# Thirty-two experts written out instead of looped, expert 1's two selections side by side, and the order of the products around gate2

## The chip, the cores and the metric

One Trainium2 chip, one of its cores. The metric is the time of one execution on the device in microseconds (us). The kernel before ran at a median of 1014.62 us over 3 runs (1013.69 to 1019.47).

## What is computed

One layer of an encoder on two requests of 256 tokens with 1024 channels (512 tokens together), all in float32. The part that matters here is its second half, a mixture of 32 experts (4 groups of 8): each token goes to the best group, and in it to the two best experts.

```python
def expert_block(args):
    xb, e = args
    return (jax.nn.silu(xb @ w_exp_gate[e]) * (xb @ w_exp_up[e])) @ w_exp_down[e]
...
x = _ln_affine(ALPHA * x + gate2 * f, ln2_g, ln2_b)
```

`w_exp_gate[e]` and `w_exp_up[e]` are 1024 x 512, `w_exp_down[e]` is 512 x 1024: 2 MB each, 6 MB for an expert, read once for each of the 32. `gate2` is a vector for each request, from its conditioning; the kernel multiplies it into the experts' results.

## The kernel before

The program is written out by hand for each engine; engines wait for each other by semaphores. After the token mixer come the router and then the experts, one after another.

**Router.** TensorE (PE) makes the router's logits (products of 36 columns), then four products of the two gate2 rows (2 rows deep, 512 columns wide) into banks 5 and 1, then `keep_clock(2)`: two full 128x128 products of 512 columns whose result nobody reads. It then waits for VectorE's (DVE's) one-hot matrix `both`, and counts, with small products, which slot of its expert each token takes. From that DVE makes `slot_of`, and from it `sel`: 0/1 matrices for a pair of experts, by which products gather an expert's up to 64 tokens.

**An expert** on PE: `gate_up` (16 products of 64 rows into bank 0, gate in the upper half, up in the lower), then `selected` (8 products that gather half of the channels of a pair of later experts into bank 2), `h_transposes` of the hidden rows, `x_transposes` of the gathered rows, then `down` (8 products into bank 1). ScalarE (ACT) applies the silu, copies `x_rows` and `hid_t` out of the banks; DVE multiplies gate by up, copies `x_t`, writes `sel` for the next pair and scales the result by gate2 (`yout`); GpSimd (POOL) stores it to `round_y`. Expert 0 gathers with float32 products (`selected_alone`). Expert 1 gathers the first half of pair (2, 3) beside its `gate_up` and the second half after its `down`, all through bank 2.

**Further rounds.** An expert may have more than 64 tokens. Behind each expert every engine reads two values from `tab` and branches over a body (`further_rounds`, on PE line 961) that is a whole second expert. With these inputs one expert of the 32 takes it.

**Loops.** PE and DVE write out experts 0 to 5, run `Fori(1, 5)` over bodies of six (experts 6 to 29; PE's loop is line 985), and write out 30 and 31. SyncE (SP) does the same from expert 6 on, ACT loops over bodies of three from expert 3, POOL over three from 0. Because a tile can't be indexed by the loop's register everywhere, DVE moves the columns of `n0` and `slot_of` down by six at the end of each body (`next_columns`, lines 1849 to 1853).

**Weights.** SP issues the loads in order. There are three buffers for gate and up, two for down:

```python
def next_gate_up(e, s):
    ...
    sp.wait_ge(m_sem["gum"], e - 2)      # gate_up of expert e-3 is done
def next_down(e, d):
    ...
    sp.wait_ge(m_sem["ym"], e - 1)       # down of expert e-2 is done
```

Both also wait until a further round of that expert is through with the buffer. Behind the loop the order is `next_down(29)`, then gate and up and down of 30, then of 31.

Of the kernel before, what the change touches and what calls it, by code (L numbers as in the profile page):

```python
# [10 lines left out]
TILES = TOK // 128  # L11
# [28 lines left out]
def hybrid_encoder(nc, x_prompt, x_sample, c_prompt, c_sample, w_mod, b_mod, w_in, b_in, w_spatial,  # L40
# [12 lines left out]
    with ctx:  # L53
# [78 lines left out]
        n0_next = at("n0_next", [128, NEXP], f32, S0 + 3072)  # L132
# [49 lines left out]
        slot_next = at("slot_next", [128, NEXP, TILES], f32, T0 + 35328)  # L182
# [174 lines left out]
        def _(sp):  # L357
# [85 lines left out]
        def _(pool):  # L443
# [150 lines left out]
        def _(pe):  # L594
# [288 lines left out]
            def down(ht, d, bank, sm):  # L883
                for fc in range(FC):
                    mm(bank[0:CAP, :], ht[:, fc, :], down_w[d][:, fc, 0:512], start=(fc == 0), stop=(fc == FC - 1))
                    x = mm(bank[CAP:128, :], ht[:, fc, :], down_w[d][:, fc, 512:1024], start=(fc == 0), stop=(fc == FC - 1))
                x.then_inc(sm["ym"], 1)

            def expert(e, k, turn, last=False, turns=None):

                s, d, a = k % 3, k % 2, k % 2
                opening = isinstance(e, int) and e == 0
                second = isinstance(e, int) and e == 1
                chooses = not (isinstance(e, int) and e >= NEXP - 2)
                loaded = 32 * (2 * turn + k // 3 + 1)
# [4 lines left out]
                pe.wait_ge(m_sem["xt"], e + 1 if opening or second else e - a + 2)  # L900
# [6 lines left out]
                if opening:  # L907
                    selected_alone(1, B[2]).then_inc(m_sem["xs"], 1)
                elif second:
                    pe.wait_ge(dve_h2lo, TILES)  # L910
                    pe.wait_ge(m_sem["sl"], 2)
                    selected(sel, B[2], 0).then_inc(m_sem["xs"], 1)
                elif chooses:
                    pe.wait_ge(m_sem["xt"], e + 2)
                    if a == 0:
                        pe.wait_ge(m_sem["sl"], 3 * turn + k // 2 + 2)
# [3 lines left out]
                if chooses:  # L920
                    pe.wait_ge(m_sem["xr"], e + 2 if opening or second else e + 3)
                    x_transposes(x_rows, B[2]).then_inc(m_sem["xtr"], 1)
                pe.wait_ge(m_sem["ht"], e + 1)
                pe.wait_ge(e_dn[d], 16 * (3 * turn + k // 2 + 1))
                if opening:
# [9 lines left out]
                if opening:  # L935
                    pe.wait_ge(dve_rt, 2)
# [7 lines left out]
            def further_rounds(e, s, d, more, first):  # L944

                def further_round(turns):
# [12 lines left out]
                    down(hid_t_x, d, B[5], x_sem)  # L959
# [30 lines left out]
            expert(30, 0, 5)  # L990
            expert(31, 1, 5, last=True, turns=last_turns)
# [21 lines left out]
        def _(act):  # L1013
# [218 lines left out]
            def rows_in(count):  # L1232
                act.wait_ge(m_sem["xs"], count)
                copy(x_rows[:, :], B[2][:, :]).then_inc(m_sem["xr"], 1)

            rows_in(1)
# [30 lines left out]
            def expert(e, turns=None):  # L1267

                opening = isinstance(e, int) and e == 0
                second = isinstance(e, int) and e == 1  # L1270
                chooses = not (isinstance(e, int) and e >= NEXP - 2)
                if opening:
                    act.wait_ge(dve_rt, 2)
                gate_silu(m_sem, B[0], sg_hid, e, 0)
                if chooses:
                    rows_in(e + 2 if opening or second else e + 3)
# [6 lines left out]
                if opening:  # L1283
# [6 lines left out]
            for k in range(3):  # L1290
                expert(k)
            with act.Fori(1, 10) as t:
                for k in range(3):
                    expert(3 * t + k)
# [46 lines left out]
        def _(dve):  # L1341
# [373 lines left out]
            def chosen_rows(out, column):  # L1715
                return dve.tensor_tensor(out[:, :, :], slots_by_tile(TILES),
# [4 lines left out]
            chosen_pair(sel, slot_of[:, 0:2, :]).then_inc(m_sem["sl"], 1)  # L1721
# [79 lines left out]
            def last_chunks(count):  # L1801
# [3 lines left out]
                columns_in(x_t[:, 1:4:2, :, :], B[2]).then_inc(m_sem["xt"], 1)  # L1805

            def expert(e, k, turn, turns=None):
                s = k % 3
                opening = isinstance(e, int) and e == 0
                second = isinstance(e, int) and e == 1  # L1810
                chooses = not (isinstance(e, int) and e >= NEXP - 2)
                dve.wait_ge(m_sem["silu"], e + 1)
                dve.tensor_tensor(sg_hid[CAP:128, :], B[0][CAP:128, :], sg_hid[0:CAP, :], ALU.mult).then_inc(m_sem["hid"], 1)  # L1813
                if opening:
# [5 lines left out]
                if s == 0:  # L1820
                    dve.tensor_scalar(side[:, 0, 0:3], n0[:, k:k + 3], -0.5, None, ALU.is_gt).then_inc(dve_g, 1)
                    dve.tensor_scalar(side[:, 1, 0:3], n0[:, k:k + 3], -0.5, None, ALU.is_le).then_inc(dve_g, 1)
                if not (isinstance(e, int) and e < 3):
                    dve.wait_ge(y_st[s], 32 * (2 * turn + k // 3))
                gate_of_slots(yout[s], dve_g, 20 * turn + 2 * (k // 3 + 1) + 2 * k, side[:, 0, s:s + 1], side[:, 1, s:s + 1])
                if opening:
                    dve.wait_ge(m_sem["xtr"], 2)
                    columns_in(x_t[:, 2:4, :, :], B[2]).then_inc(m_sem["xt"], 1)
                    chosen_pair(sel, slot_of[:, 2:4, :]).then_inc(m_sem["sl"], 1)
                elif second:  # L1830
                    first_chunks(3)
                elif chooses and k % 2 == 0:
                    first_chunks(e + 3)
                elif chooses:
                    last_chunks(e + 3)
                    chosen_pair(sel, slot_of[:, k + 3:k + 5, :]).then_inc(m_sem["sl"], 1)
                if opening:
                    for i in range(TILES):
                        dve.wait_ge(act_h2hi, i + 1)
                        dve.tensor_tensor(h2_lo[i][:, :, :], h2[i][:, :, :], h2_hi[i][:, :, :].bitcast(f32), ALU.subtract).then_inc(dve_h2lo, 1)  # L1840
                dve.wait_ge(m_sem["ym"], e + 1)
# [4 lines left out]
                further_rounds(k, *(turns or turns_of(e)))  # L1846

            def next_columns(turn):
                dve.tensor_copy(n0_next[:, 0:NEXP - 6], n0[:, 6:NEXP]).then_inc(dve_g, 1)
                dve.tensor_copy(slot_next[:, 0:NEXP - 6, :], slot_of[:, 6:NEXP, :]).then_inc(dve_g, 1)  # L1850
                dve.wait_ge(dve_g, 20 * turn + 18)
                dve.tensor_copy(n0[:, 0:NEXP - 6], n0_next[:, 0:NEXP - 6]).then_inc(dve_g, 1)
                dve.tensor_copy(slot_of[:, 0:NEXP - 6, :], slot_next[:, 0:NEXP - 6, :]).then_inc(dve_g, 1)
                dve.wait_ge(dve_g, 20 * turn + 20)

            for k in range(6):
                expert(k, k, 0)
            next_columns(0)
            with dve.Fori(1, 5) as t:
                for k in range(6):  # L1860
# [3 lines left out]
            expert(30, 0, 5)  # L1864

            chosen_rows(is_last, 1).then_inc(dve_sel, 1)
# [66 lines left out]
            expert(31, 1, 5, turns=last_turns)  # L1933
# [63 lines left out]
```

## Time and profile before

| | |
|---|---|
| profiled execution, device time | 1015.61 us |
| its span, first to last instruction | 1013.6 us |
| mean granted TensorE clock | 0.965 of full speed |
| PE matmul busy | 929.8 us (92%) |
| instructions / DMA moved | 12645 / 297.89 MB |
| token mixer and router | to about 465 us |
| experts 0 to 30 | 470.68 to 968.57 us |
| gather, last expert, layer norm, output | to 1013.6 us |

Times in rows are us from the start of the span. "issue" in the chain of waits is time in which the engine waited for nothing that the profile shows. A PE record is half of a float32 product, so 16 products show as 32 records. PEld is TensorE's weight load, and a row PEldq is an instruction of TensorE's sequencer (register work, branches). The queue q8 "instruction" carries blocks of 16 KB of program code.

### The profile page before, as it was taken

How to read it: one execution, taken by the hardware profiler on the slowest of the kernel's cores; microseconds unless marked ns; L12 is line 12 of the kernel's file. 1: busy time of each engine (PE TensorE's matmuls, PEld its weight loads, DVE VectorE, ACT ScalarE, POOL GpSimd, SP SyncE). 2: the span in 40 equal slices, each digit the busy share in tenths (PEclk: the TensorE clock that was granted, in tenths of full speed). 3: DMA queues.
4: the chain of work that ended last, by engine and by line, in shares of the span. 5: the costliest groups of instructions: out<-in, count | busy, mean ns of one | idle time of the engine just before them, and what ended most of it. 6: DMA issues, size and time to landing. Idle time of an engine off the chain costs nothing.

```text
span 1013.6 us, 12645 instructions
## 1 busy us (share of the span) xinstructions
PE 929.8 (92%) x4235; PEld 543.9 (54%) x4236; DVE 384.9 (38%) x683; ACT 244.3 (24%) x355; POOL 113.7 (11%) x174
## 2 busy tenths in 40 slices
PE   3789999999999999998999999799978899889984
PEld 2457677888888887883444344244334244344331
DVE  4522343565343257885422222222223032122235
ACT  2322243441334244363211011010010011011014
POOL 2210267000002000000000000000000000000031
PEclk9789999999999999998999999899989999899998
DMA  9884653365647525457989999999996599998953
GB/s 368 316 276 153 237 208 130 119 233 187 239 173 214 178 83 172 119 202 324 419 350 429 425 426 428 420 431 424 427 413 267 209 428 429 378 405 361 421 210 124
DMA packets 46635, 297.89 MB, mean 294 GB/s; under 512 B 4418, under 2 KB 6562, under 8 KB 30946
## 3 DMA queue, kind: packets, MB, share of 16 engines
q1 hardware_dynamic: 36352, 263.99, 64.7%
q0 software_dynamic: 9600, 31.18, 9.1%
q10 hardware_dynamic: 610, 1.66, 0.6%
q8 instruction: 57, 0.93, 0.4%
q14 instruction: 16, 0.13, 0.0%
HBM read 275.81 MB, written 21.00 MB: 293 GB/s over the span
## 4 chain that ended last, share of the span: by engine, by line
PE 84%; issue 4%; ACT 3%; DMA 3%; SPq 2%; DVE 2%; POOL 0%; DVEq 0%; POOLq 0%; ACTq 0%
PE bank L596 81%; DMA modraw<-in_w_mod 2%; PE bank L864 2%; SPq L372 2%; ACT x_rows L1015 2%; DMA y_first<-round_y,pos_y 1%; DVE wo_lo L1559 0%; PE bank L653 0%; DMA round_y<-yout 0%; ACT w_hi L1015 0%; POOL y_second L584 0%; POOL y_first L584 0%; DVE g_a L1576 0%; PE bank L880 0%; ACT L1141 0%
## 5 line engine op out<-in xcount | busy, mean ns | idle before, releaser
L596 PE MATMUL bank<-gate_w,x_t 128*64 128x512 f32 x512 | 234.0, 610 | 28.2 <-issue 26.3
L596 PE MATMUL bank<-up_w,x_t 128*64 128x512 f32 x512 | 234.4, 611 | 0.0
L596 PEld LDWEIGHTS bank<-gate_w,x_t 128*64 128x64 f32 x512 | 71.3, 141 | 176.6 <-issue 176.6
L596 PE MATMUL bank<-h_hi,w_hi 128*128 128x512 f32 x320 | 127.0, 397 | 1.6 <-ACT h_hi L1049 1.6
L596 PE MATMUL bank<-h_hi,w_lo 128*128 128x512 f32 x320 | 126.8, 396 | 0.0
L596 PE MATMUL bank<-h_lo,w_hi 128*128 128x512 f32 x320 | 125.5, 400 | 0.0
L596 PE MATMUL bank<-down_w,hid_t 128*64 128x512 f32 x512 | 116.9, 598 | 1.0 <-ACT hid_t L1015 0.9
L1813 DVE TENSOR_TENSOR sg_hid<-bank,sg_hid 64x512 f32<-64x512 f32 x32 | 22.2, 694 | 244.3 <-ACT sg_hid L1244 244.3
L1244 ACT ACTIVATE sg_hid<-bank 64x512 f32<-64x512 f32 x33 | 19.6, 592 | 376.0 <-PE bank L596 376.0
L1394 DVE TENSOR_TENSOR w_lo<-raw,w_hi 128x1024 fp32r<-128x1024 f32 x56 | 68.6, 1227 | 79.2 <-ACT w_hi L1015 79.1
L596 PEld LDWEIGHTS bank<-h_lo,w_hi 128*128 128x128 f32 x320 | 60.6, 189 | 25.3 <-issue 11.7
L538 POOL DMA_DIRECT2D round_y<-yout x31 | 16.0, 517 | 511.8 <-issue 511.8
L1015 ACT ACTIVATE w_hi<-raw 128x1024 fp32r<-128x1024 f32 x56 | 58.9, 1053 | 54.3 <-PE bank L596 51.6
L596 PEld LDWEIGHTS bank<-up_w,x_t 128*64 128x64 f32 x512 | 71.0, 141 | 0.0
L596 PEld LDWEIGHTS bank<-h_hi,w_hi 128*128 128x128 f32 x320 | 61.7, 193 | 14.3 <-ACT h_hi L1049 2.0
L596 PEld LDWEIGHTS bank<-h_hi,w_lo 128*128 128x128 f32 x320 | 61.4, 192 | 13.3
L596 PEld LDWEIGHTS bank<-down_w,hid_t 128*64 128x64 f32 x512 | 34.8, 136 | 60.4 <-issue 56.2
L1842 DVE TENSOR_TENSOR yout<-bank,yout 128x512 f32<-128x512 f32 x32 | 22.1, 691 | 82.8 <-PE bank L596 82.8
L596 PE MATMUL bank<-h_hi,sel 128*128 128x512 f32 x120 | 50.3, 419 | 0.0
L596 PE MATMUL bank<-a_lo,w_hi 128*128 128x512 f32 x128 | 49.9, 390 | 0.3 <-DVE w_lo L1394 0.3
L596 PE MATMUL bank<-a_hi,w_lo 128*128 128x512 f32 x128 | 49.8, 389 | 0.0
L596 PE MATMUL bank<-a_hi,w_hi 128*128 128x512 f32 x128 | 49.8, 389 | 0.0
(322 smaller groups left out, 1125.6 us busy)
## 6 DMA issues: line engine op xcount, KB each, us to landing
down_w<-in_w_exp_down SPq DMA_DIRECT2D x32, 2048.0 KB, 15.3
gate_w<-in_w_exp_gate SPq DMA_DIRECT2D x31, 2048.0 KB, 12.2
up_w<-in_w_exp_up SPq DMA_DIRECT2D x31, 2048.0 KB, 17.4
modraw<-in_w_mod SPq DMA_DIRECT2D x24, 1024.0 KB, 8.6
raw<-in_w_in SPq DMA_DIRECT2D x9, 2048.0 KB, 9.9
round_y<-zrow POOLq DMA_DIRECT2D x6, 2048.0 KB, 7.6
raw<-in_w_branch_b SPq DMA_DIRECT2D x2, 2048.0 KB, 9.4
raw<-in_w_branch_a SPq DMA_DIRECT2D x2, 2048.0 KB, 10.3
```

What stands on the lines that cost most here:

```text
L372: sp.dma_start(modraw0[m][:, :, :], mod_source(m)).then_inc(s_m0[m], 16)
L538: pool.dma_start(round_y[bass.ds(row, rows), 0:512], y[0:rows, :]).then_inc(done, 16)
L596: return pe.matmul(out, lhsT, rhs, start=start, stop=stop, skip_group_check=True)
L864: x = pe.transpose(bank[:, 128 * k:128 * k + 128], rows[:, 128 * k:128 * k + 128], ident)
L1015: return act.activation(out, in_, ACT.Copy, scale=scale)
L1244: act.activation(sgb[0:CAP, :], bank[0:CAP, :], ACT.Silu).then_inc(sm["silu"], 1)
L1394: dve.tensor_tensor(w_lo[par][:, :, :], raw[:, u % 2, :, 128 * (b % 4):128 * (b % 4) + 128], w_hi[par][:, :, :].bitcast(f32), ALU.subtract ...
L1813: dve.tensor_tensor(sg_hid[CAP:128, :], B[0][CAP:128, :], sg_hid[0:CAP, :], ALU.mult).then_inc(m_sem["hid"], 1)
L1842: dve.tensor_tensor(yout[s][:, :], B[1][:, :], yout[s][:, :], ALU.mult).then_inc(m_sem["yo"], 1)
```

## The change

All engines write out experts 0 to 29 one by one, with constants in place of register arithmetic; `next_columns` and its two spare tiles go. Expert 1 gathers both halves of its pair beside `gate_up`, the second into bank 6, and the transposes of the second half stand in the middle of its `down`. The first `sel` is written in two halves, so that expert 0's is there first. On PE `keep_clock(2)` moves ahead of the gate2 products, and `keep_clock(1)` stands behind them.

```diff
# SP
-            for e in range(3, 6):
+            for e in range(3, NEXP - 2):
                 next_gate_up(e, e % 3)
                 next_down(e - 1, (e - 1) % 2)
-            with sp.Fori(1, 5) as t:
-                for k in range(6):
-                    next_gate_up(6 * t + k, k % 3)
-                    next_down(6 * t + k - 1, (k + 1) % 2)
# POOL
-            with pool.Fori(0, 10) as t:
-                for k in range(3):
-                    expert(3 * t + k, k)
+            for e in range(NEXP - 2):
+                expert(e, e % 3)
# PE
+            keep_clock(2)
             for r, bank in enumerate((B[5], B[1])):
                 for c in range(2):
                     j = 2 + c
                     x = mm(bank[64 * c:64 * c + 64, :], cst[...], modrow[...])
             x.then_inc(pe_lg, 1)
-            keep_clock(2)
+            keep_clock(1)
             pe.wait_ge(dve_rt, 1)
...
-                elif second:
+                elif e == 1:
                     pe.wait_ge(dve_h2lo, TILES)
-                    pe.wait_ge(m_sem["sl"], 2)
+                    pe.wait_ge(m_sem["sl"], 3)
                     selected(sel, B[2], 0).then_inc(m_sem["xs"], 1)
+                    selected(sel, B[6], 1).then_inc(m_sem["xs"], 1)
...
-                down(hid_t, d, B[1], m_sem)
-                if second:
-                    pe.wait_ge(m_sem["xt"], 3)
-                    selected(sel, B[2], 1).then_inc(m_sem["xs"], 1)
+                down(hid_t, d, B[1], range(FC // 2))
+                if e == 1:
                     pe.wait_ge(m_sem["xr"], 4)
-                    x_transposes(x_rows, B[2]).then_inc(m_sem["xtr"], 1)
+                    x_transposes(x_rows, B[6]).then_inc(m_sem["xtr"], 1)
+                down(hid_t, d, B[1], range(FC // 2, FC)).then_inc(m_sem["ym"], 1)
...
-            for k in range(6):
-                expert(k, k, 0)
-            with pe.Fori(1, 5) as t:
-                for k in range(6):
-                    expert(6 * t + k, k, t)
+            for e in range(NEXP - 2):
+                expert(e)
# ACT, expert 1
-                if second:
-                    rows_in(4)
+                if e == 1:
+                    act.wait_ge(m_sem["xtr"], 3)
+                    rows_in(4, B[6])
# DVE
-            chosen_pair(sel, slot_of[:, 0:2, :]).then_inc(m_sem["sl"], 1)
+            for a in range(2):
+                chosen_rows(sel[:, :, a, :], a).then_inc(m_sem["sl"], 1)
...
+                elif e == 1:
+                    first_chunks(3)
+                    last_chunks(4, B[6])
+                    next_pair(4)
...
                 dve.tensor_tensor(yout[s][:, :], B[1][:, :], yout[s][:, :], ALU.mult).then_inc(m_sem["yo"], 1)
-                if second:
-                    last_chunks(4)
-                    chosen_pair(sel, slot_of[:, 4:6, :]).then_inc(m_sem["sl"], 1)
...
-            with dve.Fori(1, 5) as t:
-                for k in range(6):
-                    expert(6 * t + k, k, t)
-                next_columns(t)
```

## Rows read from the trace of the kernel before

**Rows 1.** The page: the DMA engines' busy tenths in 40 slices of the span

```profile
DMA  9884653365647525457989999999996599998953
```

**Rows 2.** The chain that ended last, from 440 us: start us, us, what

```profile
496.39 5.63 PE bank L596 x24
...
589.94 1.86 issue
591.80 9.14 PE bank L596 x40
...
616.13 12.50 PE bank L596 x56
...
629.96 12.51 PE bank L596 x56
...
647.39 6.18 issue
653.57 11.78 PE bank L596 x40
...
741.80 6.30 issue
748.11 10.63 PE bank L596 x40
...
774.65 3.61 PE bank L596 x16
...
859.79 5.96 issue
865.75 11.51 PE bank L596 x40
```

**Rows 3.** Branches of TensorE's sequencer: lines 961 and 985, ns min/median/max

```profile
L961 PEldq COMPARE_BRANCH  x32: 77/320/4337, 484.0 to 978.0; - x32
...
L985 PEldq COMPARE_BRANCH  x4: 76/7446/7641, 645.7 to 952.9; - x4
```

**Rows 4.** DMA queue of program blocks, 645 to 652 us: packets, MB, share

```profile
q8 instruction: 2, 0.03, 3.4%
```

**Rows 5.** DMA queue of the weights, 515 to 742 us: packets, MB, share

```profile
q1 hardware_dynamic: 6405, 93.36, 96.8%
```

**Rows 6.** SP's issues of the loads for down of experts 10 and 19

```profile
606.17 0.33 SPq L392 DMA_DIRECT2D down_w<-in_w_exp_down  x1
...
742.11 0.33 SPq L392 DMA_DIRECT2D down_w<-in_w_exp_down  x1
```

**Rows 7.** Us to landing of the loads issued at 513.55, 742.11, 860.10

```profile
gate_w<-in_w_exp_gate SPq DMA_DIRECT2D x1, 2048.0 KB, 7.7
...
down_w<-in_w_exp_down SPq DMA_DIRECT2D x1, 2048.0 KB, 22.9
...
down_w<-in_w_exp_down SPq DMA_DIRECT2D x1, 2048.0 KB, 17.4
```

**Rows 8.** The first products of experts 1 and 2

```profile
485.96 0.59 PE L596 MATMUL bank<-gate_w,x_t 128*64 128x512 f32 x1
...
504.53 0.61 PE L596 MATMUL bank<-gate_w,x_t 128*64 128x512 f32 x1 [1.17 <-DVE x_t L1761]
```

**Rows 9.** The router on PE and DVE, in order of time

```profile
456.53 2.72 PE L596 MATMUL bank<-modrow,cst 2*64 2x512 f32 x8
459.18 3.78 PE L596 MATMUL bank<-cst 128*128 128x512 f32 x4
...
461.52 0.29 DVE L1698 TENSOR_TENSOR both<-q,q 128x128 bf16<-128x128 f32 x1
...
464.07 0.69 DVE L1711 TENSOR_TENSOR sel<-slots,slot_of 128x512 fp32r<-128x512 f32 x1
```

**Rows 10.** Two stretches: us, PE, PEld, DVE, ACT, POOL, clock, DMA, GB/s

```profile
456.50:459.20 2.70, 2.70 (x10) 0.49 (x9) 2.25 (x11) 0.00 (x0) 0.00 (x0) 0.69 1.01 431
...
504.50:508.00 3.50, 3.47 (x10) 1.31 (x12) 0.19 (x1) 0.00 (x0) 0.00 (x0) 0.62 0.99 397
```

More of the change, by code:

```diff
@@ L881, in h_transposes, with down, expert @@
                 x.then_inc(sm["htr"], 1)
-            def down(ht, d, bank, sm):
-                for fc in range(FC):
+            def down(ht, d, bank, chunks):
+                for fc in chunks:
                     mm(bank[0:CAP, :], ht[:, fc, :], down_w[d][:, fc, 0:512], start=(fc == 0), stop=(fc == FC - 1))
                     x = mm(bank[CAP:128, :], ht[:, fc, :], down_w[d][:, fc, 512:1024], start=(fc == 0), stop=(fc == FC - 1))
[L887 to L895, printed above, removed]
+                return x
+            def expert(e, last=False, turns=None):
+                s, d, a = e % 3, e % 2, e % 2
+                loaded = 32 * (e // 3 + 1)
                 if last:
@@ L899, in expert @@
                     pe.wait_ge(e_gu[s], loaded)
-                pe.wait_ge(m_sem["xt"], e + 1 if opening or second else e - a + 2)
+                pe.wait_ge(m_sem["xt"], e + 1 if e < 2 else e - a + 2)
                 gate_up(x_t[:, 2 * a:2 * a + 2, :, :], s, B[0], m_sem, halves=(e_gu[s], loaded) if last else None)
@@ L919, in expert @@
                 h_transposes(sg_hid, B[3], m_sem)
-                if chooses:
-                    pe.wait_ge(m_sem["xr"], e + 2 if opening or second else e + 3)
+                if e < NEXP - 2:
+                    pe.wait_ge(m_sem["xr"], e + 2 if e < 2 else e + 3)
                     x_transposes(x_rows, B[2]).then_inc(m_sem["xtr"], 1)
                 pe.wait_ge(m_sem["ht"], e + 1)
-                pe.wait_ge(e_dn[d], 16 * (3 * turn + k // 2 + 1))
-                if opening:
+                pe.wait_ge(e_dn[d], 16 * (e // 2 + 1))
+                if e == 0:
                     pe.wait_ge(act_rt, 2 * TILES + 1)
@@ L1267, in expert @@
             def expert(e, turns=None):
[L1269 to L1272, printed above, removed]
+                if e == 0:
                     act.wait_ge(dve_rt, 2)
                 gate_silu(m_sem, B[0], sg_hid, e, 0)
-                if chooses:
-                    rows_in(e + 2 if opening or second else e + 3)
+                if e < NEXP - 2:
+                    rows_in(e + 2 if e < 2 else e + 3, B[2])
                 if turns is not None:
@@ L1282, in expert @@
                 hid_columns(m_sem, B[3], hid_t, e)
-                if opening:
+                if e == 0:
                     for i in range(TILES):
                         copy(h2_hi[i][:, :, :], h2[i][:, :, :]).then_inc(act_h2hi, 1)
-                if second:
-                    rows_in(4)
+                if e == 1:
+                    act.wait_ge(m_sem["xtr"], 3)
+                    rows_in(4, B[6])
                 further_rounds(*(turns or turns_of(e)))
[L1290 to L1294, printed above, removed]
+            for e in range(NEXP - 2):
+                expert(e)
             last_turns = turns_of(NEXP - 1)
@@ L1804, in last_chunks, with next_pair, expert @@
                 dve.wait_ge(m_sem["xtr"], count)
[L1805 to L1811, printed above, removed]
+                columns_in(x_t[:, 1:4:2, :, :], bank).then_inc(m_sem["xt"], 1)
+            def next_pair(first):
+                if first < NEXP:
+                    chosen_pair(sel, slot_of[:, first:first + 2, :]).then_inc(m_sem["sl"], 1)
+            def expert(e, turns=None):
+                s = e % 3
                 dve.wait_ge(m_sem["silu"], e + 1)
                 dve.tensor_tensor(sg_hid[CAP:128, :], B[0][CAP:128, :], sg_hid[0:CAP, :], ALU.mult).then_inc(m_sem["hid"], 1)
-                if opening:
+                if e == 0:
                     dve.wait_ge(dve_rt, 2)
@@ L1820, in expert @@
                 if s == 0:
[L1821 to L1826, printed above, removed]
+                    w = min(3, NEXP - e)
+                    dve.tensor_scalar(side[:, 0, 0:w], n0[:, e:e + w], -0.5, None, ALU.is_gt).then_inc(dve_g, 1)
+                    dve.tensor_scalar(side[:, 1, 0:w], n0[:, e:e + w], -0.5, None, ALU.is_le).then_inc(dve_g, 1)
+                if e >= 3:
+                    dve.wait_ge(y_st[s], 32 * (e // 3))
+                gate_of_slots(yout[s], dve_g, 2 * (e // 3 + 1) + 2 * e, side[:, 0, s:s + 1], side[:, 1, s:s + 1])
+                if e == 0:
                     dve.wait_ge(m_sem["xtr"], 2)
                     columns_in(x_t[:, 2:4, :, :], B[2]).then_inc(m_sem["xt"], 1)
[L1829 to L1837, printed above, removed]
+                    next_pair(2)
                     for i in range(TILES):
@@ L1840, in expert @@
                         dve.tensor_tensor(h2_lo[i][:, :, :], h2[i][:, :, :], h2_hi[i][:, :, :].bitcast(f32), ALU.subtract).then_inc(dve_h2lo, 1)
+                elif e == 1:
+                    first_chunks(3)
+                    last_chunks(4, B[6])
+                    next_pair(4)
+                elif e < NEXP - 2 and e % 2 == 0:
+                    first_chunks(e + 3)
+                elif e < NEXP - 2:
+                    last_chunks(e + 3, B[2])
+                    next_pair(e + 3)
                 dve.wait_ge(m_sem["ym"], e + 1)
                 dve.tensor_tensor(yout[s][:, :], B[1][:, :], yout[s][:, :], ALU.mult).then_inc(m_sem["yo"], 1)
-                if second:
-                    last_chunks(4)
-                    chosen_pair(sel, slot_of[:, 4:6, :]).then_inc(m_sem["sl"], 1)
[L1846 to L1854, printed above, removed]
-            for k in range(6):
-                expert(k, k, 0)
-            next_columns(0)
-            with dve.Fori(1, 5) as t:
-                for k in range(6):
-                    expert(6 * t + k, k, t)
-                next_columns(t)
+                further_rounds(e, *(turns or turns_of(e)))
+            for e in range(NEXP - 2):
+                expert(e)
             last_turns = turns_of(NEXP - 1)
-            expert(30, 0, 5)
-            chosen_rows(is_last, 1).then_inc(dve_sel, 1)
+            expert(30)
+            chosen_rows(is_last[:, :, :], NEXP - 1).then_inc(dve_sel, 1)
             dve.wait_ge(dve_sel, 1)
```

29 lines of the change are left out of this document (14 added, 15 removed).

## The prediction

> **What bounds the kernel now.** I read the page first, for where the DMA is full: its line stands at 9 tenths over nearly all of the expert stage, except for two slices at 760 to 811 us [rows 1]. Then the chain of waits over that stage: it is TensorE (PE) from end to end. One expert to the next takes 629.96 - 616.13 = 13.83 us where nothing disturbs it, and at 647.39, 741.80 and 859.79 PE stands still for 6.18, 6.30 and 5.96 us for nothing that the chain can name [rows 2]. These are the starts of experts 12, 18 and 24, each the first of a turn of PE's loop. The view of PE's sequencer names the cause: four branches at line 985 with a median of 7446 ns, the shortest 76 ns, which is the last one, that falls out of the loop [rows 3]; and two blocks of program code move on queue 8 just after the first of them [rows 4]. The jump back throws away the code that was fetched, and PE waits for it while its own queue runs dry. The work behind each stop is slow as well: 40 records take 11.78, 10.63 and 11.51 us where they take 9.14 behind the shorter stop at 589.94 [rows 2].
>
> Last, the weights. The stretch 515 to 742 us carries 93.36 MB on the weight queue [rows 5], 411 GB/s. An expert is three matrices of 2.097 MB, 6.29 MB, so the queue needs 15.3 us for each, more than PE's 13.83. PE is ahead of its supply, and the lag shows in the landing times, which grow while PE runs undisturbed. The stops of the loop are rests in which the supply catches up. So removing them pays only as far as the weights allow; that is the main question of this forecast.
>
> **The change part by part.** First what PE would save if the weights were always there.
>
> - Three jumps back: 6.18 + (11.78 - 9.14) = 8.8, 6.30 + (10.63 - 9.14) = 7.8 and 5.96 + (11.51 - 9.14) = 8.3 us, together 24.9 [rows 2]. Experts 0 to 5 are written out already, and in their stretch the DMA is full too; no stop of this kind stands there.
> - Forward branches over the further rounds stay, 32 of them: median 320 ns, longest 4337 [rows 3]. The one that is long at 587.9 gives the stop of 1.86 us at expert 8 [rows 2]. There are three such (experts 8, 14, 26), at one place of the loop's body, so they hang on where a block of code ends. Written out, an expert's code is a little over a block (one block of code is fetched per expert), so the place drifts, and I expect about as many, 3. Taken at 0; bounds: 3 fewer, -6 us, and 6 more, +12.
> - Expert 1: its first product starts at 485.96, that of expert 2 at 504.53, 18.57 us later [rows 8]. Beside the usual 13.83 it must hold eight more products and four transposes: the chain has `down` and the eight products of a selection at 496.39 in 5.63 us and `down` alone at 774.65 in 3.61, so these take 2.0; and the 1.33 us between 616.13 + 12.50 and 629.96 hold one ACT copy and one set of transposes, 0.7 each [rows 2]. So 16.5, a saving of 2.1. The transposes in the middle of `down` wait for ACT's copy of 0.7 us; half of `down` (1.8 us) and the wait for `hid_t` cover it, without that cover it costs 0.7. ACT's copy queues behind `hid_columns`; DVE's two column copies and the next `sel` (0.69) queue ahead of `yout`, while the second half of `down` runs, and expert 2 doesn't wait.
> - The wait of 1.17 us there is followed by a granted clock of 0.62 [rows 8, 10]: expert 2's products take 1.5 us longer than usual. With no wait this goes: 1.5.
> - The first `sel` in halves: between nothing and half of 0.69 us [rows 9]; 0.3 taken. The second half hides behind `selected_alone` of 3.65 us.
> - `keep_clock`: the gate2 records take 2.72 us at a granted clock of 0.69, so 1.9 at full; the four wide records (two products) behind them take 3.78 [rows 9, 10], at half clock as I read it, so 1.9 at full. If the clock holds, two wide products, the gate2 products and one wide one end at 456.5 + 1.9 + 1.9 + 0.9 = 461.2, before `both` at 461.81 [rows 9], and the counting starts right behind that, some 0.8 earlier than now, where it waits for the wide products to end near 462.9. If the clock falls anyway, 1.9 us of wide work less a part at full, 3.8 and 1.9 end at about 465: 2.2 later. A third way: it holds, but PE is then idle from 461.2 and the clock falls under `selected_alone`, 3.65 us that could take up to 7.3. Wide work ahead of the thin is nearest to the first case, so I take 0.8 saved, bounds 0.8 saved and 3.4 lost.
> - `next_columns` (four small copies on DVE) and the loops of ACT, POOL and SP: nothing, none is on the chain; DVE's copies hide in the 6 us stop. ACT's and DVE's branches show no long stop, in the loops or in the first experts.
>
> Together 24.9 + 2.1 + 1.5 + 0.3 + 0.8 = 29.6 us on PE.
>
> Now what the weights take back. The buffer for `down` is the tight one. Expert 10's load was issued at 606.17 and its `down` began at 629.96: 23.8 us is all that an undisturbed PE leaves [rows 2, 6]. The load for expert 19 was issued at 742.11 and took 22.9, so it landed at 765.0; its `down` began at 774.65 [rows 2, 6, 7]. That is a margin of 9.6 us only, and the DMA was full from 515 us until then. Full, it can't deliver earlier, except by what it rested before: the load of 513.55 landed after 7.7 us, into an empty queue [rows 7]; the trough before it is worth some 3 to 4 us, and the stream starts 1.1 earlier with the router and `sel`. Say 4.4, all of what expert 1 and 2 give. So expert 19 can't begin its `down` before 760.6: a gain of 14.0 us at that point, where PE alone would have 0.3 + 0.8 + 2.1 + 1.5 + 8.8 + 7.8 = 21.3. The queue takes back 7.3, in waits of up to 15.3 - 13.83 = 1.5 us before `down` from about expert 13 on.
>
> Expert 19 has the further round, a second pass of PE without new weights, and the lag clears there (the two light slices of [rows 1]). After it only the jump at expert 24 is left, 8.3. The load issued at 860.10 lands after 17.4 [rows 7]; without the stop the lag grows by 1.5 a time to about 22 at the loads for 29, under 23.8. So 8.3 less 0 to 1, 8.1 taken. The loads for 30 and 31 come in their old order behind `down` of 27 and 28 and are about due when needed. The tail from expert 30's result on is unchanged.
>
> Sum: 14.0 + 8.1 = 22.1 us. 1015.61 - 22.1 = 993.5; the profiled execution is 1.0 over the median of the runs, so 992.5.
>
> The jump is where a page and the trace are weighed. What I read in the rows is a jump that costs 7.4 us and fetches two blocks. The Trainium skill, Runtime: NRT & Kernel Launch, "Instruction fetch mechanics", says the same of a taken branch whose target is outside the fetched window, but gives TensorE's buffer as 128 KiB, or 2048 instructions. By that size a loop of six experts, at about one block of 16 KB each, would sit in the buffer, the stops would have another cause, and only 4.7 us would be gained; by the rows it is 22.
>
> **The rivals.**
>
> *The supply is faster than I think.* The margin at expert 19 assumes that nothing in the 765.0 us is slack; landing times include sharing with the stores. If the queue gives way, PE's whole 29.6 shows: 1014.6 - 29.6 = 985. Against it: 411 GB/s held over 227 us.
>
> *Forward branches stall oftener.* Nine more than before would cost 9 x 1.9 = 17 us, of which the seven before the further round fall into time that the weights take anyway. Left: 22.1 - some 8 = 14, giving 1000.5. For it: the branch over a block's end in the full queue took up to 4.3 us; against it: none of the first six.
>
> *The stops are not the jumps* but something at each sixth expert that stays. Then only 0.3 + 0.8 + 2.1 + 1.5 = 4.7 are gained: 1010. Against it: the branch that falls out of the loop takes 76 ns.
>
> *Slower than before:* the same forward branches, at nearly every expert. PE saves 29.6; to lose 0.5% (5 us) it takes 34.6 / 1.9 = 18 stops in the 24 new experts, 1020. The first six written-out experts speak against it.
>
> **How the numbers follow.** Chances: the forecast (weights take back 4 to 10 us) 0.62, faster supply 0.15, more stalls 0.14, stops stay 0.05, slower 0.02, and 0.02 for anything else that adds. A measurement tells 0.5%, 5 us, from no change: below 1009.5 is faster. The stops-stay case lies at that edge and counts as same for most of its chance. Faster 0.93, same 0.04, slower 0.03. The time is 992.5. Range 985 to 1003: down to the faster supply, and up by the router's 3.4 + 0.8, and by three further stalls after the further round, 6.
>
> **What would show it right or wrong.** The three stops of 6 us are gone and no branch takes 7 us. Between experts 13 and 19 PE waits for `down_w`, the landing times stand near 24 to 27 us there, and expert 19's `down` starts near 760. Expert 1 to 2 takes 16.5 us, with the clock at 1.00. The clock over the gate2 products is 1.00, or the router is wrong. It is wrong if the DMA moves clearly more than 411 GB/s on the weight queue, if long branches at 961 number ten, or if DVE or ACT now stop for code.

## The result and the profile after

The changed kernel ran at a median of 985.17 us (985.11 to 988.54, 4 runs) where the kernel before ran at 1014.42 (4 runs); the ratio is 0.9709, 95% interval 0.9672 to 0.9747. It is faster by 29.3 us, not by the 22.1 of the forecast: 7.3 us under the predicted 992.5, at the low end of its range. Its profiled execution took 985.14 us, its span is 983.4.

**Where it ends up.** The page's line of DMA busy tenths, against [rows 1]: the rest at 760 us is now one slice and not two.

```profile
DMA  9984663346465623809899999999999599999973
```

The chain of waits of the changed kernel, against [rows 2] (of the piece at 794.59 only the start counts here, its window ends soon after):

```profile
509.09 12.50 PE bank L589 x56
...
578.25 3.58 PE bank L589 x16
581.84 1.96 issue
583.80 10.84 PE bank L589 x40
...
678.99 0.27 issue
679.25 6.23 PE bank L589 x28
685.48 1.21 issue
686.69 6.59 PE bank L589 x28
...
698.20 3.48 issue
701.68 12.12 PE bank L589 x40
...
756.65 3.61 PE bank L589 x16
...
794.59 1.43 PE bank L589 x5
...
932.90 5.38 PE bank L589 x16
```

The stops of 6 us are gone. Two smaller ones stand at experts 8 and 16, both with slow work behind them (10.84 and 12.12 us for 40 records that take 9.14 in [rows 2]). Of two short ones, 0.27 us at expert 14 is a wait for `down_w`, and 1.21 us stands in the middle of expert 15's `gate_up`. The views of TensorE's (PE's) sequencer, of the queues from 510 to 755 us and of two loads' times to landing (issued at 655.14 and 732.80), against [rows 3 to 5, 7]:

```profile
L953 PEldq COMPARE_BRANCH  x32: 70/313/5453, 480.4 to 947.8; - x32
```

```profile
q1 hardware_dynamic: 6930, 100.91, 96.9%
...
q8 instruction: 19, 0.31, 0.5%
```

```profile
down_w<-in_w_exp_down SPq DMA_DIRECT2D x1, 2048.0 KB, 24.0
...
down_w<-in_w_exp_down SPq DMA_DIRECT2D x1, 2048.0 KB, 23.4
```

No branch takes 7 us. The weight queue carries 100.91 MB in 245 us, 412 GB/s against 411 before. The first of the two loads lands at 679.1, where `down` of expert 14 starts (679.25 in the chain); the second, for expert 19, at 756.2, and its `down` starts at 756.65. So the weights do arrive only just in time, as forecast, but the row of growing waits that was forecast between experts 13 and 19 isn't there: PE's own stops have eaten up the lead that would have turned into waits.

The rows of SyncE (SP) that answer to [rows 6], with the load of gate for expert 5:

```profile
505.91 0.33 SPq L386 DMA_DIRECT2D gate_w<-in_w_exp_gate  x1
...
732.80 0.33 SPq L390 DMA_DIRECT2D down_w<-in_w_exp_down  x1
```

The first products of experts 1 and 2, against [rows 8], and the router's products in order of time, with two windows (columns as in [rows 10]), against [rows 9, 10]:

```profile
482.36 0.59 PE L589 MATMUL bank<-gate_w,x_t 128*64 128x512 f32 x1
...
498.64 0.59 PE L589 MATMUL bank<-gate_w,x_t 128*64 128x512 f32 x1
```

```profile
454.26 1.96 PE L589 MATMUL bank<-cst 128*128 128x512 f32 x4
456.16 1.93 PE L589 MATMUL bank<-modrow,cst 2*64 2x512 f32 x8
458.02 1.13 PE L589 MATMUL bank<-cst 128*128 128x512 f32 x2
459.71 0.30 PE L589 MATMUL bank<-both,before_m 128*128 128x160 bf16 x2 [0.56 <-DVE both L1682]
```

```profile
456.40:458.00 1.60, 1.60 (x8) 0.28 (x4) 1.38 (x7) 0.00 (x0) 0.00 (x0) 1.00 0.98 420
...
497.50:501.00 3.50, 3.50 (x20) 1.15 (x16) 1.46 (x3) 0.00 (x0) 0.06 (x1) 1.00 1.00 421
```

Expert 1 to 2 takes 16.28 us with the clock at 1.00 (16.5 was forecast), and the gate2 products take 1.93 us at 1.00. In this execution these two edits do what was said of them; the router's doesn't in every one, as will be seen.

**The difference in four pieces**, from the chains of the two profiled executions:

| | before, us | after, us | gain | forecast |
|---|---|---|---|---|
| to expert 19's `down` | 774.65 | 756.65 | 18.0 | 14.0 |
| from there to expert 20's (the further round) | 39.96 | 37.94 | 2.0 | 0 |
| from there to expert 30's | 150.19 | 138.31 | 11.9 | 8.1 |
| expert 30's `down` | 3.68 | 5.38 | -1.7 | 0 |

They make 30.2, the difference of the spans (1013.6 - 983.4). So both stretches gained more than I had allowed. The runs below ask why.

### The profile page after: what moved, and what is told of

It reads as the page before. It is cut to its first block, busy times and chain, and to the rows that moved or that the text cites. A ratio compares the mean times of both kernels' runs of the same rounds, so it can differ in the third digit from the quotient of the medians.

```text
span 983.4 us, 11981 instructions
## 1 busy us (share of the span) xinstructions
PE 921.4 (94%) x4237; PEld 538.9 (55%) x4237; DVE 381.8 (39%) x662; ACT 244.0 (25%) x354; POOL 114.0 (12%) x173
## 4 chain that ended last, share of the span: by engine, by line
PE 85%; ACT 3%; DMA 3%; issue 2%; DVE 2%; SPq 2%; POOL 0%; DVEq 0%; POOLq 0%; ACTq 0%
PE bank L589 82%; DMA modraw<-in_w_mod 2%; PE bank L858 2%; SPq L370 2%; ACT x_rows L1004 2%; DMA y_first<-round_y,pos_y 1%; DVE wo_lo L1543 0%; PE bank L646 0%; DMA round_y<-yout 0%; ACT w_hi L1004 0%; PE bank L874 0%; POOL y_second L577 0%; POOL y_first L577 0%; DVE g_a L1560 0%; ACT L1130 0%
## 5 line engine op out<-in xcount | busy, mean ns | idle before, releaser
L589 PE MATMUL bank<-gate_w,x_t 128*64 128x512 f32 x512 | 229.9, 602 | 7.4 <-issue 6.7
L589 PE MATMUL bank<-up_w,x_t 128*64 128x512 f32 x512 | 230.2, 603 | 0.0
L1830 DVE TENSOR_TENSOR yout<-bank,yout 128x512 f32<-128x512 f32 x32 | 22.1, 692 | 81.9 <-PE bank L589 78.2
```

Of the source, the lines that this page charges most:

```text
L589: return pe.matmul(out, lhsT, rhs, start=start, stop=stop, skip_group_check=True)
```

## The experiments

All ratios are to the kernel before on the same chip, in rounds side by side.

### Which part of the change gives the gain

**pe_out**: the kernel before, with PE's experts alone written out.

```diff
-            for k in range(6):
-                expert(k, k, 0)
-            with pe.Fori(1, 5) as t:
-                for k in range(6):
-                    expert(6 * t + k, k, t)
+            for e in range(NEXP - 2):
+                expert(e, e % 6, e // 6)
```

> The kernel before with one edit: TensorE's experts 6 to 29 are written out; the other engines keep their loops, and the router and expert 1 stay as they were. Theory A (the jumps back of TensorE's loop cost about 8 us each with the slow clock behind them, and nothing else in the writing out matters): 24 to 25 us under the kernel before if the supply of weights keeps up, so about 990 us, no branch over 6 us but two or three of 4 to 5.5 us. Theory B (the weights were the limit, as predicted): only 17 to 18 us, about 997. Theory C (the loops of the other engines matter too): under 10 us.

989.25 us (988.24 to 991.41), ratio 0.9743 (0.9711 to 0.9774). That is the value of theory A. It doesn't decide against the weights yet: this profile has one long forward branch and the kernel before has three, a difference that is in no theory's sum.

**pe_loop**: the changed kernel with PE's loop back, the same diff the other way.

> The changed kernel with TensorE's loop over experts 6 to 29 put back and all else as changed. Theory A: the three stops of 6 us and the slow clock behind them come back, about 24 us over the changed kernel, 1009 to 1010 us. Theory C (other engines' loops matter): clearly less than 1009.

1014.8 us, ratio 0.998 (0.9959 to 1.0). Its chain has the stops of before again:

```profile
642.16 5.84 issue
648.00 11.84 PE bank L589 x40
...
737.52 5.96 issue
...
857.04 6.12 issue
```

**old_router**: the changed kernel with the router's old order.

```diff
-            keep_clock(2)
             for r, bank in enumerate((B[5], B[1])):
...
-            keep_clock(1)
+            keep_clock(2)
```

> The changed kernel with keep_clock(2) behind the gate2 products again, none ahead. If the order there is worth what the two traces show between the logits and the first selection (1.2 to 1.4 us, of which 0.3 is the halved sel): 0.8 to 1.2 us over the changed kernel, 986.2. If the 2.2 us by which the changed kernel is already earlier at the logits come from its order too: 3 us over it, 988; if they are chance of the clock at the start of the program: no more than 1.2.

984.41 us (983.11 to 989.04), ratio 0.9686 (0.9657 to 0.9716). Both expected values were higher; its interval overlaps that of the changed kernel, so no difference is seen in either direction.

**old_e1**: the changed kernel with expert 1's old order (second selection and its transposes behind `down`, through bank 2).

```diff
                     selected(sel, B[2], 0).then_inc(m_sem["xs"], 1)
-                    selected(sel, B[6], 1).then_inc(m_sem["xs"], 1)
...
-                down(hid_t, d, B[1], range(FC // 2))
-                if e == 1:
-                    pe.wait_ge(m_sem["xr"], 4)
-                    x_transposes(x_rows, B[6]).then_inc(m_sem["xtr"], 1)
-                down(hid_t, d, B[1], range(FC // 2, FC)).then_inc(m_sem["ym"], 1)
+                down(hid_t, d, B[1], range(FC)).then_inc(m_sem["ym"], 1)
+                if e == 1:
+                    pe.wait_ge(m_sem["xt"], 3)
+                    selected(sel, B[2], 1).then_inc(m_sem["xs"], 1)
+                    pe.wait_ge(m_sem["xr"], 4)
+                    x_transposes(x_rows, B[2]).then_inc(m_sem["xtr"], 1)
```

> The changed kernel with expert 1's second selection after its down again, through bank 2. If PE is the bound behind it: about 4 us over the changed kernel (2.1 of waits and 1.7 of slow clock), 989. If the supply of weights is the bound from expert 13 to 19, a later start costs less there, since the weights catch up: under 3 us.

989.28 us (986.35 to 994.14), ratio 0.9739 (0.9692 to 0.9785). The 4 us expected of a PE that sets the pace are what came, but the spread doesn't tell them from the under 3 of the other case. Two things in its profile bear on that. The slow work behind the wait in expert 2 isn't there; the piece is this (10.83 us in the kernel before):

```profile
503.68 9.14 PE bank L589 x40
```

And `selected_alone`, which this run leaves as changed, takes nearly twice its time; the changed kernel's comes second:

```profile
461.12 6.61 PE L589 MATMUL bank<-h,sel 128*64 128x512 f32 x16 [0.91 <-DVE sel L1699]
...
461.30 3.65 PE L589 MATMUL bank<-h,sel 128*64 128x512 f32 x16 [0.91 <-DVE sel L1700]
```

What follows: PE's loop is nearly everything, 27 of the 29 us when taken out alone, all but 2 of them when put back (its interval goes from nothing to 4 us). Expert 1's order is worth some 3 or 4 us by the times (989.28 - 985.17 = 4.1; 3.0 by the ratios, whose intervals overlap), and 2.3 us by the traces: from expert 0's first product to the load for expert 5 it is 41.1 us in `old_e1` and in `pe_out`, 38.8 with the new order. The slow clock behind the wait, another 1.7 us, is there in the kernel before and in `before_light` and isn't in these two, though the wait is. And 3.0 us of what `old_e1`'s profile lost come from `selected_alone`. The router's order is worth nothing that can be measured. Writing out the other engines is worth nothing that shows either: `old_e1` has it, `pe_out` hasn't, and both take 989.3; the forecast had it so.

### How much the weights take back

**only19**: the changed kernel with the code of the further round (reading `tab`, the branch and the body) on PE, ScalarE and VectorE behind expert 19 alone, where these inputs need it. No forward branch is left elsewhere.

```diff
-                further_rounds(e, s, d, *(turns or turns_of(e)))
+                if e == 19:
+                    further_rounds(e, s, d, *(turns or turns_of(e)))
```

> The changed kernel with the further-round code on PE, ACT and DVE only behind expert 19, the one that takes it with these inputs; the other 31 branches and bodies go, and the result is the same. It takes away the stops for code at experts 8, 15 and 16 of the changed kernel (1.96 + 1.7, 1.5, 3.5 + 3.0 us with the slow clock behind them, some 11.6 us). Theory W (the weight queue bounds the stretch up to expert 19 as predicted, and the stops were hidden in front of it): the time stays within 3 us of the changed kernel, PE waits for down_w from about expert 12 on, and expert 19's down starts at 755 to 757. Theory P (PE is the bound there): about 11 us less, near 974.

983.22 us (981.3 to 985.98), ratio 0.9699 (0.9666 to 0.9733). The chain has stops of PE right before `down`, and no others:

```profile
662.22 0.36 issue
...
676.49 1.04 issue
...
691.45 1.36 issue
692.81 7.46 PE bank L589 x25
```

Later ones (722.25, 2.00; 753.71, 0.79) are of the same kind. The waits for `down_w` that I had forecast are here, growing from expert 13 to 15 by the size forecast (up to 1.5 us each, with one of 2.0), and each ends 0.1 us behind the landing of its load; in the changed kernel PE's own stops take their place.

**light**, **only19_light**, **before_light**: the changed kernel, `only19` and the kernel before, each with only half of every `down` matrix loaded from expert 2 on, 5.24 MB for an expert instead of 6.29 (products as before, over what the buffer holds).

```diff
-                sp.dma_start(down_w[d][:, :, :], gate_src(w_exp_down, e)).then_inc(e_dn[d], 16)
+                if e < 2:
+                    sp.dma_start(down_w[d][:, :, :], gate_src(w_exp_down, e)).then_inc(e_dn[d], 16)
+                else:
+                    sp.dma_start(down_w[d][:, 0:2, :], gate_src(w_exp_down, e)[:, 0:2, :]).then_inc(e_dn[d], 16)
```

> The changed kernel with the half loads for down (half of each down matrix is left out, as in only19_light). Its waits for weights were 0.3 us in the profile of the changed kernel, so if only waits count, at most 1 us less than the changed kernel. If a full DMA also lengthens the fetch of code, the long branches get shorter and it is 2 to 5 us less.

974.4 us (971.79 to 980.21), ratio 0.9601 (0.957 to 0.9632). That is 10.8 us less than the changed kernel, and both of my cases were wrong: I had counted the waits in its profile (0.3 us) and not the stops that hid the queue's limit. The profiled execution is the slowest of the four; it has two long forward branches.

> The same, and the loads for down of experts 2 to 31 bring only half of the matrix; the products use what lies in the other half, so that part of the result is left out. An expert then needs 5.24 MB, 12.8 us at 411 GB/s, less than PE's 13.83. Both theories: no wait for weights, 972 to 975. What only19 takes over this is what the weights take back: 7 to 11 us by W, about 0 by P.

973.84 us (973.64 to 973.91), ratio 0.9604 (0.9577 to 0.963).

> The kernel before with the half loads for down (half of each down matrix left out). PE never waited for weights there, so the time stays within 1 us if the length of a jump back doesn't depend on the DMA. If the full DMA lengthens the fetch of code, the three jumps of 7.4 us get shorter, and it is 3 to 8 us less.

1014.17 us, ratio 1.0002 (0.9985 to 1.0018). The jumps back cost as much as before, though the queue moved 83.89 MB between 510 and 755 us and not a hundred:

```profile
L988 PEldq COMPARE_BRANCH  x4: 76/7026/7614, 646.2 to 952.4; - x4
```

What follows: the kernel before doesn't wait for weights at all. With the weights out of the way the change gives 1014.17 - 974.4 = 39.8 us, where my sum for PE was 29.6. And the weights take back 985.17 - 974.4 = 10.8 us, where my sum was 7.3 + 0.2. The pair without forward branches spreads less and gives 983.22 - 973.84 = 9.4; its two profiles reach expert 19's `down` at 754.50 and 745.08, 9.4 apart as well, so all of it is taken before that mark. Both terms were too small, and they have opposite signs.

### Does the queue decide when expert 19 starts?

**after_again**: the changed kernel a second time, unaltered. **late3** and **late8**: the changed kernel, where the load of gate for expert 3 also waits for an event on PE (`late3`: the end of expert 0's selection; `late8`: of its `down`), so that the stream of weights starts later while PE's work stays.

```diff
                 sp.wait_ge(m_sem["gum"], e - 2)
                 sp.sem_inc(sp_go, 1)
+                if e == 3:
+                    sp.wait_ge(m_sem["xs"], 2)      # late8: m_sem["ym"], 1
+                    sp.sem_inc(sp_go, 1)
```

> The changed kernel, not altered: a second profile and time. Every theory expects 985, within 3 us, with span marks the same. It shows how much of the 3.6 us by which the weights' stream started earlier than in the kernel before is chance of one execution (the router's sum at 454.5 against 456.6 us): if the part before the router is chance, this mark varies between 453 and 457 without following the kernel.

986.97 us (984.87 to 989.81, 6 runs), ratio 0.973 (0.9701 to 0.9759).

> The changed kernel, but the first load that has to wait for a buffer (gate of expert 3, issued at 474.43 us in the changed kernel) also waits until expert 0's selection is done, about 477.6 us. Nothing on TensorE moves by itself. Theory 'the queue decides when expert 19 starts': the loads run back to back from here; a rest of about 0.9 us before the load of 505.91 is lost first, so everything behind comes about 2.3 us later (3.2 less 0.9), less the 0.45 us by which expert 19's weights were early: its products for down start at about 758.5 instead of 756.65, and the time is about 987. Theory 'the queue has slack, only code and TensorE decide': expert 19 stays at 756 to 757, 985.2.

986.38 us (983.88 to 988.32, 6 runs), ratio 0.972 (0.9691 to 0.975).

> The changed kernel, but the same load of gate of expert 3 waits until expert 0's products for down are done, about 482.8 us: 8.4 later. Theory 'the queue decides': 8.4 less the 0.9 us rest and the 0.45 us margin, expert 19's down starts at about 763.7 and the time is about 992, which is the blind forecast; part of it shows as waits for down_w that replace TensorE's stops for code. Theory 'the queue has slack': 985 to 986, as nothing else is later.

993.97 us (988.64 to 997.4, 6 runs), ratio 0.9791 (0.9754 to 0.9827).

The second execution of the changed kernel reaches expert 19 by another way. Its chain:

```profile
662.10 1.34 issue
...
677.36 1.64 issue
...
723.42 2.33 issue
...
741.03 14.30 PE bank L589 x56
...
756.66 3.58 PE bank L589 x15
...
839.10 2.40 issue
841.50 9.15 PE bank L589 x40
```

It has no stop at expert 8 and none at 16, and waits before `down` instead; expert 19's `down` starts at 756.66, in the first profile at 756.65. In one execution there are 1.96 + (10.84 - 9.14) + 1.21 + 3.48 + (12.12 - 9.14) = 11.3 us of stops and slow work, in the other waits for weights. That the mark differs by 0.01 us only is luck: the load lands at 756.2 and 755.9, and PE gets there 0.4 and 0.8 us later. But it lands at the same time within 0.3 us, and PE can't begin sooner; the queue sets the floor.

`late8` issued the load for expert 3 at 482.97 instead of 474.43. Its chain at expert 19, and the landing time of that expert's load, issued at 737.60:

```profile
761.75 0.87 issue
```

```profile
down_w<-in_w_exp_down SPq DMA_DIRECT2D x1, 2048.0 KB, 24.9
```

The load lands at 762.5, `down` starts at 762.62: 5.97 later, and the time is 7.0 over that of the changed kernel beside it. Expected were 763.7 and 7. `late3` issued the load at 477.34, 2.9 later, and expected 2.3; but its `down` starts at 756.80 and its time is not longer. So some 2.6 us of a delay are lost on the way (8.54 - 5.97), not the 1.35 that I had put in (0.9 and 0.45), and the rest shows in full. Where they are lost isn't shown. It is not in rests of the queue, as I had thought: the changed kernel has none behind the load of 474.43, the DMA share is 0.97 to 1.03 in each 5 us from 475 to 515 us. What counts is when the stream starts again after the router's stretch, and whether it rests later. The kernel before does rest once more, ahead of the load of 513.55 [rows 7]. The window 510 to 515 us, before and after (columns as in [rows 10], the last three are clock, DMA share, GB/s):

```profile
510.00:515.00 5.00, 5.00 (x24) 2.46 (x20) 0.99 (x2) 0.59 (x1) 0.00 (x0) 1.00 0.39 115
...
510.00:515.00 5.00, 5.00 (x26) 1.65 (x24) 0.69 (x1) 0.00 (x0) 0.00 (x0) 1.00 1.01 429
```

### Where the long forward branches stand

**pad64**: the changed kernel with 64 more semaphore instructions on PE.

```diff
+            for _ in range(64):
+                pe.sem_inc(pe_go, 1)
             pe.sem_inc(x_sem["ym"], 1)
             pe.sem_inc(x_sem["gum"], 1)
```

> The changed kernel with 64 more semaphore instructions at the start of TensorE's program, in a stretch where TensorE waits for its first data anyway, so all of its code behind them lies 64 instructions further. If the long forward branches (4 to 5.5 us, at experts 7, 15 and 22 or 23 in the executions so far) come from where an expert's branch lies against the ends of the blocks of code, they move to other experts, about two earlier; their number stays at 2 to 4 and the time within 3 us of the changed kernel's. If they come from chance in the fetching alone, they stay at the same experts or come at random. No theory expects a cost of the instructions themselves.

997.93 us (994.21 to 1001.12, 6 runs), ratio 0.9833 (0.9803 to 0.9864). This expectation holds a mistake of mine: the place is not at the start of the program but right ahead of expert 0, on PE's path. The chain, with the stop that this makes, and the next one:

```profile
466.53 9.01 issue
475.54 4.65 PE bank L589 x13
...
564.04 2.00 issue
566.05 10.84 PE bank L589 x40
```

```profile
L953 PEldq COMPARE_BRANCH  x1: 4179/4179/4179, 561.7 to 561.7; - x1
```

The stop is 9.01 us where the changed kernel has none, 0.14 us for each of 64. The time is 11.0 us longer than the changed kernel's beside it (986.97); PE and the queue both move, so nothing hides it. That these instructions cost anything, no theory of mine had. What was asked can still be read, for the code behind lies 64 instructions further. The one long branch stands behind expert 5. In the eight profiles that have the branches, written-out PE code and no shift (`pe_out`, `old_router`, `old_e1`, `light`, `late3`, `late8` and the changed kernel twice) they stand behind experts 7, 15 or 23 and nowhere else: 4, 6 and 2 times. The shift moves the place by two experts, as expected, by this one profile with its one long branch (2 to 4 were expected); a place eight experts apart is what fits a piece of code that drifts against fixed boundaries by the same amount for each expert. Which of the three places stalls in an execution is not settled; 12 in eight profiles is 1.5 each. In the loop (before, `before_light`, `pe_loop`) they stood behind 7, 13 and 25 in all three profiles: 3 each.

## Why the forecast was right and wrong

**Right: what bounds the kernel, and the jump back.** The stops of 6 us are PE's loop: out with it alone, 27 us go; back with it alone, they return. The rival that the stops are something else is out. With it goes what I had drawn from the buffer size of the Trainium skill (Runtime: NRT & Kernel Launch, "Instruction fetch mechanics"), that a loop of six experts sits in it, with a gain of 4.7. The section doesn't say that a buffer of this size spares a jump back the fetch, and the runs disagree with that inference: the branch took 6.9 to 7.6 us each time it was taken. They don't measure the size.

**Right: expert 1's waits, the other engines' loops.** 2.3 us against 2.1; nothing against nothing. The dip of the clock behind the wait (1.5 forecast, 1.7 between the two profiles) is there in two of four profiles that have the wait: a term that the edit gains in some executions only. That the times gave 4.1 against a forecast of 3.9 is in part luck.

**Not settled: the router.** In the changed kernel's profile the clock held, and from the logits' sum to expert 0's first product it took 12.61 us instead of 14.05. But of the ten profiles with the new order, two (`old_e1` and `pe_loop`) have the third way of the forecast: `selected_alone` takes 6.6 us at a granted clock of 0.55, and the stretch 15.6 us. In three others the wide products ahead take 3.3 to 3.5 us and not 1.96, and the stretch 13.5. The four profiles with the old order have 3.65 us for `selected_alone` each time and 13.9 to 14.5 for the stretch. So the new order gains 1.4 us in some executions and loses as much in others, and the old order in the changed kernel measures the same time. What is gained or lost there does move the start of the weights' stream: `old_router`'s profile starts expert 0 2.4 us later than the changed kernel's and expert 19's `down` 1.9 us later, at 758.5.

**Wrong, first step: "Forward branches over the further rounds stay ... Taken at 0".** I reasoned that as many would be long, 3, and left the lower bound of -6 us unused. On average half as many are (1.5), and those before expert 19 cost nothing, since the queue decides there. After expert 19 the profile of before had one, in expert 26: a stop of 2.43 and 0.7 us of short stops and slow work next to it, 3.1 of the 3.8 by which the last stretch gained more than forecast. Most of what is left is a stop of 0.57 us ahead of expert 30 (954.51 in the chain of before). The sum for PE was too small for the same reason: 39.8 measured with light weights against 29.6, and 1014.17 - 973.84 = 40.3 without any forward branch. In the chain of before, the three forward stops and the short ones next to them cost 8.0 us over the usual 13.83 for each expert. So they are the larger part of the 10.7 that are missing against 40.3; the rest I can't place within the spread of those runs.

**Wrong, second step: "So expert 19 can't begin its `down` before 760.6".** It began at 756.65, 0.4 us behind the landing of its weights: the queue is the limit, as said, at 412 GB/s, as said. What was off is mainly when the full stream starts. I let it start 1.1 us earlier and added 3.3 for the trough. Measured: the load for expert 19 lands at 756.2 and not 765.0, 8.8 us earlier and not 4.4. The stream starts again with the load of 474.43 where it was 478.03 before, 3.6 us earlier and not 1.1. The trough was sized about right: the share of 0.39 in the window above and 0.89 in the one behind it make 3.6 us of rest, and the changed kernel has none. The 1.6 us left I can't place. Of the 3.6 of the start, the router gives 1.4, and 2.2 stand ahead of the router: the logits' sum is at 454.47 instead of 456.63. The change touches nothing there. In the thirteen other profiles that mark lies between 452.8 and 456.1, `before_light` at 454.16 and the second execution of the changed kernel at 454.30: it is chance of the execution, and the profile of before was the latest of all. It helps the table above, not the medians.

**The rival that has the number is not what happened.** "The supply is faster than I think" gives 985, and 985.17 came. But its mechanism was a queue that gives way until PE's 29.6 show. The queue didn't give way: it took back some 10 us, from a PE that had saved some 40. Two sums that were both too small by 3 and 10 left a difference that is right for the rival by accident. Without the light kernels I'd have taken the number for a proof.

**Left to chance.** The further round gained 2.0 (39.96 to 37.94), and 36.6 us were enough for it in `after_again` and `late3`; `late8` took 39.7. In between, the same products take 3.9 or 5.5 us. In expert 30 the changed kernel lost 1.7 in the same way (a granted clock of 0.66 from 933 to 938 us). Why PE's clock falls in one execution and not in another at the same place isn't settled.

**Tried for a better kernel.** None here beats the changed one for any input: `only19` (983.22) knows where the further round is, and its interval overlaps. The light kernels show what there is to win: 10 us, if the queue had fewer bytes or earlier room before expert 19.

## What to carry to other kernels

When two resources are nearly even, cost both with the other taken away, and only then subtract: here a sum of 29.6 less 7.5 stood for 39.8 less 10.8. Ask for each stretch which of the two decides at its end; what the other one loses before that mark (11 us of stops here) costs nothing as long as it doesn't make the first one start later, as `late8` did. An order that keeps the clock up in one profile must be looked at in several. And a loop whose body is long can cost its jump back in full on the engine that sets the pace, about 8.3 us a turn in this kernel; look for it at the first place where the profile says that an engine waited for nothing.

## What the runs showed of the hardware that I had not expected

- A jump back over six experts' code takes 6.9 to 7.6 us with the weight queue at 97% and at 86% (`before_light`, 510 to 755 us): it doesn't shorten when a sixth of the bytes go.
- The long forward branches may: behind expert 15 it takes 4.2 us in `light` and 4.6 to 5.5 us in five profiles with all weights; behind expert 7 it's 4.0 against 4.1 to 4.3. That is too few to tell.
- A long forward branch comes at fixed places of the written-out code, eight experts apart, but only in about half of the cases where it could (12 of 24).
- With the same instructions `selected_alone` takes 3.65 us at a granted clock of 1.00 in eight of ten profiles and 6.6 us at 0.55 in two, each time behind a wait of 0.9 us.
- 64 semaphore increments in PE's queue cost 9 us, 0.14 us each: not free on the engine that sets the pace.
- From execution to execution the end of the token mixer moves by 3.8 us (452.8 to 456.6), for the same instructions.
